# Turning the residual rows for the router by SBUF transfers and VectorE, in place of TensorE

## The reference

```
xp = xp + merge_heads(pool_o, attn, w_out)          # mixer output product, added to the residual
n  = rms_norm(x, norm_ffn)                           # channel_mixer
hf = n.astype(float32)                               # hier_moe: D_MODEL = 1024
p_group  = softmax(hf @ w_group)                     # 4 groups
logits_e = (hf @ w_expert).reshape(T, 4, 8)          # 32 experts, 8 a group
# best group, top 2 experts in it, gates; then every expert (1024 -> 512 -> 1024) on its rows
```

## Time and profile before

| | |
|---|---|
| time, median of 3 runs | 1084.18 us (1082.72 to 1085.72) |
| the profiled execution's own time | 1081.97 us |
| its span in the trace | 1080.2 us |
| PE busy | 1038.2 us (96%) |
| DVE busy | 542.3 us (50%) |
| ACT busy | 306.2 us (28%) |
| POOL busy | 173.5 us (16%) |
| moved by DMA | 293.19 MB, mean 271 GB/s |

### The profile page before, as it was taken

How to read it: one execution, slowest core, us unless ns; L and a number is a source line. 1 busy time by engine, 2 the same in 40 slices (tenths; PEclk the granted TensorE clock), 3 DMA queues, 4 the chain that set the end, 5 groups by cost and what they waited for, 6 DMA issues and landing times.

```text
span 1080.2 us, 29154 instructions
## 1 busy us (share of the span) xinstructions
PE 1038.2 (96%) x12741; PEld 824.6 (76%) x12741; DVE 542.3 (50%) x1060; ACT 306.2 (28%) x588; POOL 173.5 (16%) x155
## 2 busy tenths in 40 slices
PE   8999999999999989999999999999999989889896
PEld 7999999977666559989867898656898557556565
DVE  6326664558875544345644454455445434343431
ACT  6323332356775552213311101110111010101011
POOL 0001200599300000100101111111111111101102
PEclk9999999999999999999999999999999999999999
DMA  7357785000126468676999999999999999999993
GB/s 250 111 163 210 221 269 163 1 14 3 39 73 202 119 233 298 222 264 222 349 390 390 378 388 380 395 385 376 374 381 387 380 389 389 387 391 392 391 388 102
DMA packets 85816, 293.19 MB, mean 271 GB/s; under 512 B 13425, under 2 KB 44849, under 8 KB 60069
## 3 DMA queue, kind: packets, MB, share of 16 engines
q1 hardware_dynamic: 78277, 273.30, 67.7%
q0 software_dynamic: 7280, 17.58, 6.9%
q10 hardware_dynamic: 128, 0.39, 0.1%
HBM read 272.98 MB, written 42.87 MB: 292 GB/s over the span
## 4 chain that ended last, share of the span: by engine, by line
PE 77%; DMA 15%; DVE 3%; SPq 2%; ACT 1%; issue 1%; POOL 0%; ACTq 0%; POOLq 0%
PE bank L2871 22%; DMA w_all<-in_w_up 15%; PE bank L2415 12%; PE bank L2651 8%; PE bank L2458 4%; PE bank L2888 4%; PE bank L2586 3%; PE bank L2623 3%; PE bank L2892 3%; PE bank L2496 3%; SPq L1058 2%; PE bank L2896 2%; PE bank L2518 1%; PE bank L2737 1%; PE bank L2411 1%; DVE keep L1926 1%
## 5 line engine op out<-in xcount | busy, mean ns | idle before, releaser
L2871 PE MATMUL bank<-w_all,xeT 128*32 128x256 f32 x6144 | 347.5, 383 | 20.8 <-DMA w_all<-in_w_up 17.6
L2871 PEld LDWEIGHTS bank<-w_all,xeT 128*32 128x32 f32 x6144 | 256.0, 111 | 105.5 <-issue 27.7
L2242 DVE STREAM_TRANSPOSE xeT<-xg 32x256 f32<-32x256 f32 x360 | 156.5, 435 | 91.5 <-DMA xg<-n_scr,tab 86.3
L2888 PE MATMUL bank<-w_all,hT 128*32 128x256 f32 x744 | 165.6, 379 | 0.0
L2892 PE MATMUL bank<-w_all,hT 128*32 128x512 f32 x744 | 129.3, 592 | 0.0
L1926 DVE TENSOR_TENSOR_SCAN keep<-keep,unseen 128x1024 f32<-128x1024 f32 (+7 forms) x64 | 95.8, 1529 | 33.7 <-ACT keep L1450 33.7
L2415 PE MATMUL bank<-w_hi,xh 128*128 128x256 f32 x376 | 108.1, 287 | 0.1
L2415 PE MATMUL bank<-w_hi,xl 128*128 128x256 f32 x376 | 105.5, 281 | 0.0
L2415 PE MATMUL bank<-w_lo,xh 128*128 128x256 f32 x376 | 105.5, 280 | 0.0
L2888 PEld LDWEIGHTS bank<-w_all,hT 128*32 128x32 f32 x744 | 81.8, 110 | 30.3
L1697 ACT ACTIVATE sgl<-bank 128x384 f32<-128x384 f32 x32 | 15.7, 491 | 304.0 <-PE bank L2871 304.0
(11 more groups left out here) (316 smaller groups left out, 1485.0 us busy)
## 6 DMA issues: line engine op xcount, KB each, us to landing
w_all<-in_w_down SPq DMA_DIRECT2D x64, 1024.0 KB, 30.2
w_all<-in_w_gate SPq DMA_DIRECT2D x64, 1024.0 KB, 30.8
w_all<-in_w_up SPq DMA_DIRECT2D x64, 1024.0 KB, 31.4
k_scr<-in_cache_k SPq DMA_DIRECT2D x32, 256.0 KB, 3.1
v_scr<-in_cache_v SPq DMA_DIRECT2D x32, 256.0 KB, 3.5
pgk<-k_scr SPq DMA_DIRECT2D x32, 256.0 KB, 4.0
w_raw<-in_w_in SPq DMA_DIRECT2D x7, 1024.0 KB, 6.7
pgv<-v_scr SPq DMA_DIRECT2D x4, 1024.0 KB, 5.8
```

The costliest lines, as they stand in the source:

```text
L2242: last = dve.transpose(xeT[i][rows_of(s), :, rows_of(g)], lane[:, :, s, :])
L2871: lasts = [pe.matmul(pair_ps(i)[rows_of(q), g, :, :], xeT[i][:, k, rows_of(g)], pair_of(b, i, k, q), start=(k == 0 and g != 1), stop=(k == ...
L2888: return pe.matmul(y_right_ps(g), hT[:, ft, rows_of(g)], w[ft // 2][:, ft % 2, DA:D], start=first and g != 1, stop=ends, skip_group_check= ...
```

## The change

For tiles 0 to 6 (`LANED = LAST - 1 = 7`) PE's eight turns and ACT's copy are gone. In their place the finished tile is copied inside SBUF to `lanes_in`, so that each 32-partition lane l holds columns 256 l to 256 l + 255 of all 128 rows: 16 transfers a tile of 32 partitions x 256 columns (32 KB each), eight issued by SP behind the tile's store, eight by ACT ahead of the tile's squares. VectorE then turns all 32x32 squares of the tile in one instruction into `nT` (`turn_lanes`), between add (1, t+1) and add (2, t+1). This turn leaves the columns on partitions in another order, so POOL copies `w_r` once into `w_l` in that order, in 16 linked copies. Tiles 7 and 8 keep the old way. `lanes_in` is one buffer, so transfers of tile t wait for the turn of tile t - 1.

```diff
+    LANED = LAST - 1
+    SIDE = P // 4
+    LCOLS = D // 4
+    LANE_DMAS = 16 * 16
+    lanes_in, _ = place("lanes_in", [P, P // SIDE, LCOLS], F32, at_late)
+    w_l, at = place("w_l", [P, KT, NGRP + NE], F32, at_b)
...
@@ SP @@
+            def rows_to_lanes(t):
+                if t >= 1:
+                    sp.wait_ge(s_n2c, t)
+                for g in (0, 1):
+                    for l in range(4):
+                        sp.dma_start(lanes_in[SIDE * l:SIDE * l + SIDE, g, :],
+                                     xmid[SIDE * g:SIDE * g + SIDE, t, LCOLS * l:LCOLS * l + LCOLS]).then_inc(s_lane, 16)
...
                 store_residual(t)
+                if t < LANED:
+                    rows_to_lanes(t)
                 sp.wait_ge(s_wo, tile_done(t))
                 load_part((0, 1, 3, 4)[t // 2], (t % 2,))
                 if t == 5:
                     sp.wait_ge(s_yst, 16 * (t + 1))
-                    sp.wait_ge(s_n2T, t + 1)
+                    sp.wait_ge(s_lane, LANE_DMAS * (t + 1))
...
@@ POOL @@
-            pool.tensor_tensor(w_r[:, :, :], w_r[:, :, :], gain, ALU.mult).then_inc(s_wg, 1)
+            chain.link(pool.tensor_tensor(w_r[:, :, :], w_r[:, :, :], gain, ALU.mult))
+            for l in range(4):
+                for s in range(4):
+                    move = pool.tensor_copy(w_l[SIDE * l:SIDE * l + SIDE, :, :].rearrange("p (y s) e -> p y s e", s=4)[:, :, s, :],
+                                            w_r[SIDE * s:SIDE * s + SIDE, 2 * l:2 * l + 2, :])
+                    if (l, s) != (3, 3):
+                        chain.link(move)
+            move.then_inc(s_wg, 1)
...
@@ ACT @@
+            def rows_to_lanes(t):
+                act.wait_ge(s_xm, tile_done(t))
+                if t >= 1:
+                    act.wait_ge(s_n2c, t)
+                for g in (2, 3):
+                    for l in range(4):
+                        act.dma_start(lanes_in[SIDE * l:SIDE * l + SIDE, g, :],
+                                      xmid[SIDE * g:SIDE * g + SIDE, t, LCOLS * l:LCOLS * l + LCOLS]).then_inc(s_lane, 16)
...
             for t in range(LAST):
-                if t >= 1:
-                    copy_turned(t - 1)
+                if t < LANED:
+                    rows_to_lanes(t)
                 square_mid(t)
                 root_mid(t)
...
@@ DVE @@
+            def turn_lanes(t):
+
+                dve.wait_ge(s_lane, LANE_DMAS * (t + 1))
+                if t >= 2:
+                    dve.wait_ge(s_lgp, t - 1)
+                dve.transpose(nT[t % 2][:, :, :].rearrange("p k (g r) -> p g k r", r=SIDE), lanes_in[:, :, :]).then_inc(s_n2c, 1)
...
                 dve.tensor_tensor(dst, out_ps(s)[0:r, :], dst, ALU.add).then_inc(s_xm, 1)
+                if n == 1 and 1 <= t <= LANED:
+                    turn_lanes(t - 1)
...
@@ PE @@
-                    last = pe.matmul(logit_ps(t)[0:r, :], nT[t % 2][:, k, 0:r], w_r[:, k, :],
+                    last = pe.matmul(logit_ps(t)[0:r, :], nT[t % 2][:, k, 0:r], (w_l if t < LANED else w_r)[:, k, :],
...
                 out_product(s)
                 n, t = wsteps[s]
-                if n == 1 and t >= 1:
-                    transpose_mid(t - 1)
                 if n == NO - 1 and t >= 1:
                     logits(t - 1)
```

More of the change, by code:

```diff
@@ L297, in hybrid_step @@
     assert at <= at_t
+    LANED = LAST - 1
[4 more added lines that the diff above has]
+    w_l, at = place("w_l", [P, KT, NGRP + NE], F32, at_b)
+    assert at <= at_t
     gffn, at = place("gffn", [P, D], F32, at_u)
@@ L312, in hybrid_step @@
     row_oh, = table(at_x2, at_a, (("row_oh", [P, 2, NB, CAP], F32),))
-    at_tmp = at_late + 4 * 2 * NB * (CAP + 2 * NE)
+    at_tmp = at_late + 4 * D
     rhs, prod, tmp32, ek, le = table(at_tmp, at_yo_end, (
@@ L521, in hybrid_step @@
     s_xs = sem("x_normed")
-    s_xT = sem("x_transposed")
+    s_xT = sem("x_transposed_then_last_residual_rows_transposed")
     s_xh = sem("x_hi_ready")
@@ L589, in hybrid_step @@
     s_n2 = sem("ffn_normed")
-    s_n2T = sem("ffn_transposed")
+    s_lane = sem("residual_rows_in_lanes")
     s_n2c = sem("ffn_copied")
@@ L1104, in _ @@
                     sp.wait_ge(s_yst, 16 * (t + 1))
-                    sp.wait_ge(s_n2T, t + 1)
+                    sp.wait_ge(s_lane, LANE_DMAS * min(t + 1, LANED))
+                    if t == 7:
+                        sp.wait_ge(s_xT, NT + 1)
                     if t == 3:
@@ L1225, in _ @@
             gain = gain_ffn[:, :].rearrange("p (k x) -> p k x", x=1).to_broadcast([P, KT, NGRP + NE])
-            pool.tensor_tensor(w_r[:, :, :], w_r[:, :, :], gain, ALU.mult).then_inc(s_wg, 1)
+            chain.link(pool.tensor_tensor(w_r[:, :, :], w_r[:, :, :], gain, ALU.mult))
[6 more added lines that the diff above has]
+            move.then_inc(s_wg, 1)
+            pool.wait_ge(s_wg, 1)
             chain.link(pool.memset(ones[:, :], 1.0))
@@ L1631, in copy_turned @@
                 r = ROWS[i]
-                act.wait_ge(s_n2T, i + 1)
-                if i >= 2:
-                    act.wait_ge(s_lgp, i - 1)
+                act.wait_ge(s_xT, NT + i + 1 - LANED)
+                act.wait_ge(s_lgp, i - 1)
                 act.activation(nT[i % 2][:, :, 0:r], norm_ps(i)[:, :, 0:r], ACT.Copy).then_inc(s_n2c, 1)
+            def rows_to_lanes(t):
[6 more added lines that the diff above has]
+                                      xmid[SIDE * g:SIDE * g + SIDE, t, LCOLS * l:LCOLS * l + LCOLS]).then_inc(s_lane, 16)
             def square_mid(t):
@@ L2141, in turn_copied @@
                 r, k = ROWS[LAST], TURNS[part]
-                dve.wait_ge(s_n2T, NT + part)
+                dve.wait_ge(s_xT, NT + NT - LANED + part)
                 dve.wait_ge(s_lgp, LAST - 1)
                 dve.tensor_copy(nT[LAST % 2][:, k, 0:r], last_norm_ps(part)[:, :, 0:r]).then_inc(s_n2c, 1)
+            def turn_lanes(t):
[3 more added lines that the diff above has]
+                dve.transpose(nT[t % 2][:, :, :].rearrange("p k (g r) -> p g k r", r=SIDE), lanes_in[:, :, :]).then_inc(s_n2c, 1)
             def scale_logits(t):
@@ L2743, in transpose_mid @@
                 pe.wait_ge(s_xm, tile_done(t) - (1 if KT - 1 not in ks else 0))
-                if t >= 1 and ks[0] == 0:
+                if ks[0] == 0:
                     pe.wait_ge(s_n2c, t)
@@ L2748, in transpose_mid @@
                     last = pe.transpose(out, xmid[0:r, t, k * P:(k + 1) * P], ident[0:r, 0:r])
-                last.then_inc(s_n2T, 1)
+                last.then_inc(s_xT, 1)
             def ranks(q):
```

## The result

The changed kernel takes 1112.74 us (median of 4 runs, 1110.11 to 1115.49), the kernel before 1083.99 us (4 runs, 1082.72 to 1085.72). The ratio is 1.0269, 95% interval 1.0249 to 1.0288: 28.8 us slower, where 7.7 us were forecast and 1103 us was the upper end of the range.

What follows compares the result with a forecast made beforehand. The weight stream ends the kernel and starts full behind the row stage, paced by PE in light tiles. Row stage: 10.7 us lost, 3.0 gained, 7.7 slower: 1089.7 us, median 1091.9; range for 8 in 10 1083 to 1103.

Steps and rivals of the forecast that it cites:

- late tiles: Row stage, tiles 0, 3, 5 and 6: DVE's gap becomes the longer one; 1.8, 3.5, 1.8 and 3.6 us lost.
- Eight at 0.46 us, the last one shorter, make 3.6 us.: ACT, ahead of each tile's squares and root: issuing eight transfers delays DVE's chain by 3.6 us unless slack takes it.
- upper end of this step: ACT's eight issues at the full queue's 1.04 us each, 8.3 us; as a rival 1124 us, chance 0.05.
- the prediction's own formula: Each tile's gap is the longer of DVE's, start of add (1, t+1) as before + 5.95 us, and PE's.
- becomes the old one less 1.0: PE, tiles 0 to 6: without the eight turns its gap from tile to tile shrinks by 1.0 us.
- light tiles: Row stage, tiles 1, 2 and 4: PE 10.03 us against DVE 9.86 still sets the pace; 1.0 us gained each.
- This is the new coupling: DVE: logits need the turn, which stands behind add (1, t+1), so lateness after tiles 3 and 6 now holds PE.
- the removed turns: PE: dropping eight turns frees 1.0 us a tile, 7.0 us over seven tiles if nothing else binds.
- SP's issues hidden: SP: issuing store and eight transfers takes about 4.0 us; weight halves go back 3.7 us a tile at no cost.
- POOL's copies hidden: POOL: 16 copies end at 441 to 447.7 us, first logits start about 447.0; at most 0.7 us lost, taken as 0.
- the lanes hidden in the changed kernel: Last lane lands at a + 6.7 to 8.4 us, turn starts at a + 8.2 in light tiles; 1.5 us cover at best.
- the third rival: Lanes land late: last transfer needs 6 us instead of 2.6; 6 us more, 1098 us; chance 0.15.

Runs made afterwards that it cites:

- the kernel with TensorE kept at work: Changed kernel, with TensorE multiplying the identity by itself ahead of the router's products while it would wait for the turn: 1107.85 us, ratio 1.0227.
- the four-load kernel: Changed kernel with four loads a tile on SP from the tile's stored rows in HBM instead of sixteen transfers, ScalarE issuing none: 1100.8 us, ratio 1.0162.

## Why the prediction was wrong

The direction and the mechanism held: row stage sets the start of the full weight stream, ScalarE's issues push the root back, DVE's chain behind the root becomes the pace, and the late tiles lose most. Three steps failed, the first by far the most.

**"Eight at 0.46 us, the last one shorter, make 3.6 us."** Measured: 5.4 to 7.1 us, 42.6 instead of 25.2 us over the stage. The price came from rows of loads out of HBM; a transfer inside SBUF takes 0.62 to 0.64 us to issue at the median, which makes some 5.1 us for eight, and single issues up to 1.6 us make the rest. I had 8.3 us as the upper end of this step, but gave it 0.05 and nothing in between. With the measured holds the prediction's own formula gives gaps of 14.5, 11.7, 12.5, 16.3, 12.4, 15.1 and 19.0 us, 101.5 in sum: 24.7 of the 27.9 us. The formula is some 0.3 us too long in each gap (for the kernel with TensorE kept at work it gives 101.5 too, and 99.6 were measured); with that taken off it explains 22.7 us, and the clock's 5.1 are the rest.

**PE's gap "becomes the old one less 1.0".** That can hold at full clock only. Tiles 1 and 4 took 13.8 and 14.9 us, since PE came back from waits of 6.0 and 4.1 us at half clock; kept at work the kernel lost 4.6 us less in all. At full clock these tiles took 11.4 and 12.2 us, which is DVE's chain with the real hold: the 0.17 us by which PE was to set the light tiles' pace were gone too. The prediction named waits of 4 to 5 us for PE and did not ask what they do to the clock.

**"This is the new coupling" (the turn behind the late add).** Only in part. A hold of 5.4 us without turn and without transfer costs 16.8 us, since add (2, t+1) stands behind the same add. What the turn adds in the late tiles is about its own length: 16.11 against 15.12 us behind tile 3 (both engines issuing, TensorE turning), and 1.1 us in tiles 0, 3 and 6 alike once the two kernels' holds are set off. Since the formula had the whole chain in it, the number did not suffer.

Right, by their rows: the turn (1.24 us forecast from its rows, 1.24 measured, half of the 2.5 us estimated beside it), the removed turns (0.9 us in the one tile where nothing else binds, tile 2 of the four-load kernel), SP's issues hidden, POOL's copies hidden (PE waited for the turn, not for `w_l`), the lanes hidden in the changed kernel (no wait of the turn for a transfer). The last is right for the wrong reason: ScalarE's hold made the turn so late that the lanes were there. With the issues behind the root the third rival is true: the last transfer needs 6 us, by the look of it because it stands behind the weight half. The Trainium skill, "DMA: Bandwidth & Descriptors", section "Issuing engines are not separate DMA queues", says that a second issuing engine only saves the sequencer's time and that this is usually small beside the transfer. For one transfer the trace does not speak against it (0.63 us to issue, 2.4 us to landing), but it misleads for eight in a row: on ScalarE their time was the most of the loss, and on SP it cost nothing.

No version here beats the kernel before. A turn and a router product one tile later, with two lane buffers, might take the landing off the path; it was not tried.

## What to carry to other kernels

Price a transfer first by what its issue does to the engine that issues it: the same eight cost nothing measurable on an engine that nobody waits for and 18 us on one that stands between a tile and its chain. Work out for each pass of the loop how much hold its slack covers (here 1.3 to 6.1 us without the turn) and expect nothing below it and the rest above. Look at what is issued just ahead of a small transfer that somebody waits for: behind a 1 MB load it took 6 us to land where its neighbours took 2. And when a change makes TensorE wait several us, add the slow clock behind the wait to the bill.

## What the hardware showed that was not expected

- An issue of a transfer with both ends in SBUF: 0.59 to 0.64 us median, on SP and on ScalarE, 32 x 256 or 128 x 64; from HBM, 32 x 256, 0.45 us. Two engines issuing at the same time did not slow each other (0.62 us and 5.6 to 7.6 us for ScalarE's eight, against 0.62 and 5.3 to 7.1 alone).
- A 32 KB transfer inside SBUF, issued 0.3 us behind a 1 MB load by another engine: 5.1 to 6.4 us to landing, against 1.9 to 3.1 at the median for those of the same tile ahead of the load (landings counted in the order of issue).
- TensorE at a granted clock of 0.50 behind a wait of 6 us, which nearly doubled the router's products from 1.87 to 3.63 us.
- A 512 KB store to HBM issued right behind two 1 MB loads by the same engine: 10.7 us until the next transfer that waited for it could be issued, 6.7 us a tile before.
